# ScalarE's place in a bisection search beside a product: 5 counts for two units in place of 6, weight rounding among the last counts, and the 1024-key tile moved to ScalarE

## What is computed

```python
def dsa_attention(q, k, v, qi, ki, wi, pos, topk):
    def block(args):
        qb, qib, wib, t = args
        sc = jnp.einsum('bqhd,bsd->bqhs', qib, ki).astype(jnp.float32)
        idx_score = jnp.einsum('bqhs,bqh->bqs', jax.nn.relu(sc), wib.astype(jnp.float32))
        causal = t[:, None] >= pos[None, :]
        idx_score = jnp.where(causal[None], idx_score, -jnp.inf)
        _, idx = lax.top_k(idx_score, topk)
        ...
```

## Time and profile before

| | us |
|---|---|
| median of 3 runs (lowest, highest) | 3175.38 (3171.77, 5718.26) |
| the profiled execution, its own time | 3177.37 |
| its span | 3176.0 |
| PE busy in the span | 2864.3 (90%) |
| DVE busy | 1655.6 (52%) |
| ACT busy | 1048.4 (33%) |
| POOL busy | 733.2 (23%) |

### The profile page before, as it was taken

One profiled execution on the slowest core, in us unless ns is written; L12 is line 12 of the kernel. 1 busy time (PEld: TensorE's weight loads), 2 busy tenths in 40 slices (PEclk: granted clock), 3 DMA queues, 4 the chain that ended last, 5 costly groups with the idle time before them and its releaser, 6 DMA issues. The chain is left out here.

```text
span 3176.0 us, 39052 instructions
## 1 busy us (share of the span) xinstructions
PE 2864.3 (90%) x14802; PEld 2326.5 (73%) x14802; DVE 1655.6 (52%) x2848; ACT 1048.4 (33%) x2082; POOL 733.2 (23%) x458
## 2 busy tenths in 40 slices
PE   6999678989999999989798999889897888999988
PEld 4768577778888888867386787667684777877767
DVE  4270686534223233333888653575336797534855
ACT  3150555120000001111584540463005664421751
POOL 1233103213333333332021203203130213014021
PEclk9999778999999999999999999899899999999989
DMA  3111002111111111131111003104320220022032
GB/s 104 41 33 40 1 1 78 66 41 37 45 60 40 53 54 50 57 121 37 34 66 48 1 1 102 32 19 159 125 62 2 66 71 11 1 65 69 1 133 93
DMA packets 78972, 168.33 MB, mean 53 GB/s; under 512 B 15024, under 2 KB 33984, under 8 KB 78272
## 3 DMA queue, kind: packets, MB, share of 16 engines
q1 hardware_dynamic: 70336, 140.61, 13.6%
q10 hardware_dynamic: 8448, 25.18, 2.9%
HBM read 128.00 MB, written 20.97 MB: 47 GB/s over the span
## 5 line engine op out<-in xcount | busy, mean ns | idle before, releaser
L332 PE MATMUL psum<-H,ffn_W 128*128 128x512 f32 x672 | 262.8, 391 | 4.8 <-DVEq L1779 3.1
L334 PE MATMUL psum<-H,ffn_W 128*128 128x512 f32 x672 | 262.4, 390 | 0.0
L333 PE MATMUL psum<-H,ffn_W 128*128 128x512 f32 x672 | 262.4, 390 | 0.0
L2019 DVE TENSOR_SCALAR_CACHE_REDUCE MB<-OM,tk_mid 128x512 bf16<-128x512 f32 (+2 forms) x192 | 184.3, 1010 | 2.3
L518 POOL TENSOR_TENSOR tk_W<-tk_W 128x1024 fp32r<-128x1024 f32 (+1 forms) x38 | 76.6, 2019 | 422.2 <-ACT tk_W L470 422.2
L1546 POOL CAST ffn_W<-ffn_W 128x1024 fp32r<-128x1024 f32 (+1 forms) x77 | 65.1, 846 | 471.4 <-PE psum L334 468.8
L1988 ACT ACTIVATE MB<-OM,tk_mid 128x384 bf16<-128x384 f32 (+2 forms) x192 | 157.0, 819 | 49.1 <-DVE tk_mid L2016 44.5
L1760 DVE TENSOR_SCALAR ffn_Y<-ffn_G,ffn_par 128x1024 f32<-128x1024 f32 x21 | 21.5, 1022 | 288.2 <-ACT ffn_G L1733 288.2
L1733 ACT ACTIVATE ffn_G<-psum 128x1024 f32<-128x1024 f32 x21 | 21.6, 1031 | 445.9 <-PE psum L334 445.9
L1548 POOL TENSOR_TENSOR ffn_W<-ffn_W,ffn_W 128x1024 fp32r<-128x1024 f32 (+1 forms) x77 | 152.7, 1983 | 6.2
L332 PEld LDWEIGHTS psum<-H,ffn_W 128*128 128x128 f32 x672 | 126.8, 189 | 32.6 <-POOLq L1619 3.5
(11 more groups left out here) (453 smaller groups left out, 7579.4 us busy)
## 6 DMA issues: line engine op xcount, KB each, us to landing
OM<-in_w_feat SPq DMA_DIRECT2D x34, 512.0 KB, 4.5
tk_W<-in_w_feat SPq DMA_DIRECT2D x22, 512.0 KB, 3.6
ffn_W<-in_ffn_w_gate SPq DMA_DIRECT2D x21, 512.0 KB, 3.5
ffn_W<-in_ffn_w_val SPq DMA_DIRECT2D x21, 512.0 KB, 3.6
ffn_W<-in_ffn_w_down SPq DMA_DIRECT2D x42, 256.0 KB, 2.6
OM<-MB ACTq DMA_DIRECT2D x64, 128.0 KB, 2.5
OM<-OM ACTq DMA_DIRECT2D x64, 128.0 KB, 3.4
fin_W<-in_w_out SPq DMA_DIRECT2D x4, 2048.0 KB, 10.3
```

The costliest lines, as they stand in the source:

```text
L332: pe.matmul(out, a1, b1, start=start, stop=False)
L333: pe.matmul(out, a1, b2, start=False, stop=False)
L334: return pe.matmul(out, a2, b1, start=False, stop=stop)
L2019: own(dve.tensor_scalar(MB[:, self.keys(t)], IS[:, self.keys(t)], mid[:, n:n + 1], 0.0, ALU.is_lt, ALU.add, accum_out=self.cnt[:, n:n + 1]))
```

## The change

Three edits. ACT's turn of unit n now comes after 5n // 2 + 2 rounds, so that after the last unit 27 rounds are done and not 32. The six last roundings of the wide product's items, which stood behind all rounds, now stand among the last five: one behind round 28, one behind 30, one behind 32, then three. And the tile of 1024 keys (t = 7) is counted by ACT, the one of 896 (t = 6) by DVE.

```diff
--- before.py
+++ after.py
@@ -474,7 +474,7 @@
                         round_on_act(i)
                 for n, u in enumerate(by_act):
                     if beside:
-                        beside.count_on_act(act, min(BISECTIONS, 3 * n + 2))
+                        beside.count_on_act(act, min(BISECTIONS, 5 * n // 2 + 2))
                     act.wait_ge(products, u + 1)
                     if beside and u + PARTS < len(items):
                         round_on_act(u + PARTS)
@@ -486,9 +486,10 @@
                         act.wait_ge(taken_act, by_act.index(u) + 1)
                         act.dma_start(*units[u].store).then_inc(stored[stores.index(u) % 2], 16)
                 if beside:
+                    for n, i in enumerate(range(len(units) + PARTS, len(items))):
+                        beside.count_on_act(act, min(BISECTIONS, 5 * len(units) // 2 + 2 * n + 1))
+                        round_on_act(i)
                     beside.count_on_act(act, BISECTIONS)
-                    for i in range(len(units) + PARTS, len(items)):
-                        round_on_act(i)
                 for n, wide in enumerate(wides):
                     for t in range(NT):
                         if t < NT - 1:
@@ -1961,8 +1962,8 @@
 class TopK:
 
 
-    ON_ACT = (2, 4, 6)
-    ON_DVE = (3, 5, 7)
+    ON_ACT = (2, 4, 7)
+    ON_DVE = (3, 5, 6)
 
     def __init__(self, kit, mem, IS, AM, MB, B, R, causal):
         nc = kit.nc
```

## The result

The changed kernel takes 3188.06 us in the median of six runs (3186.74 to 3190.83), the kernel before 3177.72 beside it. The ratio is 1.0039 [1.0027, 1.005], so the change costs 12.4 us (8.6 to 15.9). The two medians lie 10.3 apart; the ratio is that of the fast executions alone, and one of before, of 5718.26, is a slow one. The forecast was +7.8 with 3183, and a range of 3175 to 3191. The profiled execution took 3186.74, its span is 3185.3.

What follows compares the result with a forecast made beforehand. The search set the pace until 1700, then PE's wide product ended the stage; DVE's selection would end it after the change. 1.8 + 3.0 + 3.0 = 7.8 us slower, 3183 for the median, 8 in 10 from 3175 to 3191.

Steps and rivals of the forecast that it cites:

- Which chain ends the stage: End of the search stage: DVE's selection ends it at 1750.0 in layer 1, the product being done at 1736.4.
- The turns and the start of the wide product: Layer 1: wide product starts at 1692.1, 9.1 us earlier; PE pauses 2 us, not 11; five rounds are left.
- Edit 1: Exchange of the 1024-key and 896-key tiles: DVE saves 0.13 us a round, alone at most 4.2 us of counting.
- The DVE chain, "+1.8 and +3.0": Search and selection on DVE: the next stage starts 1.8 us later in layer 1, 3.0 later in layer 2.
- about 5.7: First item of the wide product on PE: about 5.7 us and not 8.39, if the clock stays at 2.4 GHz.
- twice the mean: Upper bound on DVE's selection: each POOL subtraction costs twice the mean 0.79 us, so it ends at 1753.
- The clock at the entry, "I take 1.5": Start of the sparse attention: PE's cold clock costs 0 to 2.4 us, taken as 1.5, 3.0 for two layers.
- The rival that the clock stays down: Sparse attention: clock at 0.50, 9.6 us more PE work a layer, half on the path; 3190 us. Chance 0.15.
- The sum: Whole kernel: 1.8 + 3.0 for the two layers' chains and 3.0 for PE's clock, together 7.8 us slower.
- The rival "even": Search ends 2 to 3 us earlier than forecast or POOL hits little, entry warm enough: 3174 to 3179. Chance 0.2.
- What I said would be seen of ACT: Sign in ACT's timeline: its idle time moves to waits for PE.

Runs made afterwards that it cites:

- short_sel_after: The changed kernel without the selection for row tiles 5, 6 and 7; 3156.63 us, ratio 0.9936 against the kernel before.
- short_sel_before: The kernel before without the selection for row tiles 5, 6 and 7; 3176.49 us, ratio 0.9993 against the kernel before.
- thr_only: The kernel before with the 5n // 2 + 2 rounds alone, tiles and late roundings as before; 3185.47 us, ratio 1.0037 against the kernel before.
- plan: The kernel before with listed rounds ahead of each turn, 3, 7, 10 and so on to 30, ahead of the last; 3158.21 us, ratio 0.9952.
- swap_only: The kernel before with only the 896-key and 1024-key tiles exchanged between ACT and DVE; 3174.38 us, ratio 1.0001 against the kernel before.
- bank_wait: The changed kernel with PE waiting bank by bank for the units' copies at the wide product's start; 3182.57 us, ratio 1.0017 against the kernel before.
- pe_warm17: The changed kernel with 17 idle matmuls on PE behind the wide product; 3183.86 us, ratio 1.0021 against the kernel before.
- late_round: The changed kernel with the six last roundings behind rounds 30, 31, 32, 32, 32, 32; 3182.8 us, ratio 1.0028 against the kernel before.
- pe_warm: The changed kernel with 64 idle matmuls on PE behind the wide product, outlasting the selection; 3265.98 us, ratio 1.0279 against the kernel before.
- plan_again: The same kernel as plan, run again in another group; 3159.21 us, ratio 0.9936 against the kernel before.
- three_four: The kernel before with 3n + 4 rounds ahead of unit n's turn in place of 3n + 2; 3161.46 us, ratio 0.9952 against the kernel before.
- plan_bank: The kernel before with rounds 5, 8, 10 and so on to 31 ahead of turns, plus bank-by-bank wait; 3151.45 us, ratio 0.9915.

## Why the prediction was right, and where its sizes were off

**Which chain ends the stage: shown.** It was the step on which the sign rested, and short_sel_after and short_sel_before prove it on both sides.

**The turns and the start of the wide product: right.** Forecast 1692.1, measured 1692.95 - 0.74 = 1692.21; PE's pause was 2.5 and not 2.0. Unit 10 is done at 1692.95 - 2.53 - 0.74 = 1689.7, ACT comes to it at 1691.15 - 0.74 = 1690.4 (forecast 1690.3), and five rounds are left, all as forecast. thr_only, with five left and neither of the other edits, has most of the loss, and plan, with two left, has none.

**Edit 1: right.** A round "3.59" takes 1707.10 - 1703.51 = 3.59. Alone the edit was given at most 4.2 us, "less where a turn makes ACT late", and swap_only measures nothing.

**The DVE chain, "+1.8 and +3.0": mis-sized by 4.1 and 4.2 us.** Measured were 5.8 and 7.3. That the measured time still lies in the range is the range's width; each of four small terms came out longer, none shorter. In layer 1, with the 0.74 taken off, the keep of round 28 is at 1695.3 and that of the last round at 1714.56, where 1711.75 was forecast. The 2.8 us between, and what follows, are:

- Item 11, forecast as "about 5.7" with the clock at 2.4 GHz, took 1700.30 - 1692.95 = 7.35. The term that failed is the first item's time, and in it the choice that the clock stays up over the pause. Counts of round 29 started at 1700.84 - 0.74 = 1700.1 and not at 1698.3: +1.8. bank_wait, without pause and cold item, has 5.64.
- The `mid` ahead of round 31 took 1.25 in place of 0.23, since POOL's subtraction had started 0.07 us before: +1.0. The prediction priced such blocking in the selection and left it out of the rounds.
- The selection took 1754.57 - 1715.30 = 39.27 and not 38.2: +1.1. Four subtractions fell into it, as forecast, and cost 1.05 each where 0.79 was taken. As a length that is within the bound of "twice the mean" (35.07 + 4 x 1.58 = 41.4); the bound on the end, 1753, didn't hold, since the end is 1754.57 - 0.74 = 1753.8 behind a keep that came 2.8 late.
- The barrier took 0.55 and not 0.32, because DVE now comes last to it: +0.2.

A subtraction of POOL and the operations that it met, kernel after, timelines of POOL and of DVE:

```profile
1707.49 1.29 POOL L519 TENSOR_TENSOR tk_W<-tk_W 128x512 fp32r<-128x512 f32 x1 [5.18 <-ACT tk_W L470]
...
1723.52 1.81 POOL L519 TENSOR_TENSOR tk_W<-tk_W 128x512 fp32r<-128x512 f32 x1 [4.90 <-ACT tk_W L470]
```

```profile
1724.21 2.20 DVE L2044 TENSOR_TENSOR_SCAN OM<-tk_one,OM 128x512 f32<-128x512 bf16 x1
```

The 6-column `mid` ends at 1708.81, POOL's subtraction at 1708.78: the small operation stood until the large one was done. The Trainium skill ("SBUF — State Buffer", Who interferes with whom) says that whoever has the shared pair holds the other off fully, and names tensor_scalar among those that can need it; the trace agrees, with 1.02 us of 1.29 lost. By this rule the prediction would have had 2.0 us more in the selection of each layer, by the mean of before none; 1.1 came.

**The clock at the entry, "I take 1.5": measured 0.83 by pe_warm17**, 1.85 for both layers by the lengths of before and after in place of 3.0. The sign and the place were right. The rival that the clock stays down also saw its premise fulfilled, a PEclk of 0.53 over 20 us in place of 0.83. Its price did not follow. The 9.6 us of added PE work that I worked out for it, half of it on the path, showed as under 1 us. The likely reason, argued from PE's busy share of 12.26 in 20 us and not tested, is that the gaps between PE's pieces took it up; pe_warm17, with 10 us at 0.50 behind its warm start, is at most 0.2 us longer there than before.

**The sum.** Forecast 7.8 = 1.8 + 3.0 + 3.0. By the lengths it is 5.8 + 7.3 + 1.85 = 14.9, by the ratio 12.4. The chain was forecast 8.3 too small and the clock's part 1.15 too large; the two errors offset only slightly. The rival "even" fell with the chain: it wanted the search's end 2 to 3 us earlier than forecast, and it came 2.8 later. What I said would be seen of ACT, that its idle time moves to waits for PE, was half right: the waits for PE in front of its roundings rose from 14 to 20 but fell in sum, from 75.7 to 60.4. The wait that grew is DVE's for ACT, from 33.1 to 69.7, and I had not named it as a sign.

## What to carry to other kernels

Work that is tied to another engine's pace gets done only while it is tied: when a turn is moved forward to serve PE, count how much of the slower chain is left behind the last turn, and what that chain still has to do afterwards. Put nothing that waits for the other chain ahead of work that the longer chain waits for: the first late rounding put two rounds later and the second put one later were together worth 3 us a layer. And if a wait for a whole resource (all PSUM banks) is the reason for a turn to be early, first try to wait for the part that is written next, which took the pause away with no move of a turn (bank_wait, 3.7 to 4.0 us a stage).

## What the runs showed of the hardware that was not expected

- A short pause can cost the clock. Of twelve starts of the wide product behind a pause of 2.4 to 2.5 us (after, thr_only, late_round, short_sel_after, pe_warm, pe_warm17, two layers each), the granted clock went to 0.50 within 2 us in eleven, for about 3 us; in one of these, layer 2 of short_sel_after, it had fallen when PE restarted, in the others it fell behind the restart. Behind 1.9 us (plan and plan_again) it stayed at 1.00 in layer 1 and fell in layer 2, both times; behind 3.6 us (three_four) it fell in both. Windows of plan, layer 1 and 2:

```profile
1689.00:1692.00 3.00, 3.00 (x14) 2.47 (x14) 1.15 (x5) 2.48 (x6) 0.00 (x0) 1.00 0.77 262
2585.00:2588.00 3.00, 3.00 (x8) 2.35 (x8) 1.36 (x6) 2.24 (x7) 0.00 (x0) 0.50 0.57 182
```

  With no pause (bank_wait, plan_bank) it stayed at 1.00 in all four. The Trainium skill ("TensorE: Matmul & The Clock Gate", HAM oscillation) tells of a matmul loop that starts cold behind each of its waits for a load. These traces agree in part: most of these starts lost the clock, but most of them began at 1.00 and lost it 1 to 2 us later, and three, layer 2 of late_round and layer 1 of plan and plan_again, never did.
- A DVE operation of 6 columns can be held for the whole of a POOL subtraction of 512 columns: 0.23 us became 1.25.
- A PEclk far lower over the first 20 us of the sparse attention (0.53 for 0.83) cost 1 us at most in after. It is not so everywhere: layer 1 of thr_only and layer 2 of plan lost the clock a second time some 16 us behind the entry, and have the longest sparse attention of the table, 88.01 and 87.19 us. The second fall of thr_only:

```profile
1763.00:1766.00 3.00, 1.28 (x11) 0.96 (x10) 1.71 (x5) 2.95 (x6) 2.43 (x2) 1.00 0.00 0
1766.00:1769.00 3.00, 3.00 (x14) 2.08 (x15) 0.58 (x2) 2.34 (x5) 0.00 (x0) 0.50 0.00 0
```
